# The projection's operand splits made during the gate products of the state-space stage

## The reference

```
proj = jnp.einsum('ntd,de->nte', h, lw['w_in'])
q, kc, vc, ks, vs, kw, vw, g_nsa, u, g_a, g_s = jnp.split(proj, offs, axis=-1)
...
z = jax.nn.gelu(y)
out = z * jax.nn.sigmoid(z @ w_glu.astype(f32))
```

## Time and profile before

| | us |
|---|---|
| median of 3 runs | 2201.22 |
| lowest and highest | 2199.24, 2216.53 |
| the profiled execution | 2202.53 |
| its span in the trace | 2200.7 |
| TensorE matmuls busy | 2053.4 (93%) |
| DVE, ACT, POOL busy | 904.2, 768.3, 559.5 |

### The profile page before, as it was taken

One profiled execution on the slowest core, in us unless ns is written; L12 is line 12 of the kernel. 1 busy time (PEld: TensorE's weight loads), 2 busy tenths in 40 slices (PEclk: granted clock), 3 DMA queues, 4 the chain that ended last, 5 costly groups with the idle time before them and its releaser, 6 DMA issues.

```text
span 2200.7 us, 33694 instructions
## 1 busy us (share of the span) xinstructions
PE 2053.4 (93%) x13952; PEld 1846.2 (84%) x13952; DVE 904.2 (41%) x1719; ACT 768.3 (35%) x1557; POOL 559.5 (25%) x455
## 2 busy tenths in 40 slices
PE   6998899799989999686999999999999999999997
PEld 4765599788766677455999998999999999999997
DVE  4773311166576777374211133453124214313414
ACT  5132311255466777343322232333023113202313
POOL 0640000255244444222212221122122122112120
PEclk9989899799978999798999999999999999999999
DMA  9204134465132232767111113111111111111122
GB/s 361 89 1 123 41 73 104 126 238 197 71 77 78 63 87 63 258 258 282 48 48 49 47 50 108 39 43 45 49 49 39 49 49 39 49 49 40 47 58 79
DMA packets 217072, 201.54 MB, mean 92 GB/s; under 512 B 38198, under 2 KB 199966, under 8 KB 208264
## 3 DMA queue, kind: packets, MB, share of 16 engines
q1 hardware_dynamic: 205126, 131.40, 20.9%
q0 software_dynamic: 9216, 67.11, 7.9%
q10 hardware_dynamic: 2578, 0.88, 0.2%
HBM read 177.62 MB, written 21.58 MB: 91 GB/s over the span
## 4 chain that ended last, share of the span: by engine, by line
PE 51%; DMA 1%; DVE 0%; ACT 0%; SPq 0%; issue 0%; ACTq 0%; DVEq 0%
PE ps L2230 17%; PE ps L2228 17%; PE ps L2229 17%; PE ps L2374 1%; DMA tail<-in_w_in 1%; DMA tail<-x_keep 1%; PE ps L2395 0%; DVE tail L2739 0%; ACT tail L2568 0%; DVE tail L2715 0%; SPq L2340 0%; SPq L2353 0%; ACT tail L2559 0%; DVE tail L2657 0%; ACT tail L2473 0%
## 5 line engine op out<-in xcount | busy, mean ns | idle before, releaser
L2228 PE MATMUL ps<-tail,tail 128*128 128x356 f32 (+2 forms) x2304 | 757.5, 329 | 12.3 <-POOL tail L2626 9.5
L2230 PE MATMUL ps<-tail,tail 128*128 128x356 f32 (+2 forms) x2304 | 751.1, 326 | 0.0
L2229 PE MATMUL ps<-tail,tail 128*128 128x356 f32 (+2 forms) x2304 | 749.2, 325 | 0.0
L2626 POOL TENSOR_TENSOR tail<-tail,tail 128x1024 fp32r<-128x1024 f32 x96 | 232.2, 2419 | 927.7 <-ACT tail L2473 927.7
L2228 PEld LDWEIGHTS ps<-tail,tail 128*128 128x128 f32 x2304 | 436.1, 189 | 15.3 <-POOL tail L2626 9.7
L2229 PEld LDWEIGHTS ps<-tail,tail 128*128 128x128 f32 x2304 | 436.2, 189 | 2.6 <-issue 0.2
L2230 PEld LDWEIGHTS ps<-tail,tail 128*128 128x128 f32 x2304 | 436.3, 189 | 0.0
L2473 ACT ACTIVATE tail<-tail 128x1024 fp32r<-128x1024 f32 x96 | 101.0, 1053 | 323.1 <-PE ps L2230 314.6
L2657 DVE SCALAR_TENSOR_TENSOR tail<-ps,mod,tail 128x346 f32<-128x346 f32 (+2 forms) x120 | 68.7, 572 | 347.7 <-PE ps L2230 337.7
L1683 POOL TENSOR_SCALAR pr<-pr,row_reciprocals,gT 128x640 f32<-128x640 f32 (+7 forms) x128 | 98.8, 781 | 145.0 <-DVE row_reciprocals L1809 142.4
L2528 ACT ACTIVATE tail<-tail,tail 128x346 f32<-128x346 f32 (+2 forms) x96 | 56.0, 583 | 195.5 <-DVE tail L2697 100.2
(11 more groups left out here) (492 smaller groups left out, 2987.8 us busy)
## 6 DMA issues: line engine op xcount, KB each, us to landing
tail<-in_w_ff SPq DMA_DIRECT2D x64, 512.0 KB, 3.9
wada_late<-in_w_ada SPq DMA_DIRECT2D x32, 512.0 KB, 4.1
wada<-in_w_ada SPq DMA_DIRECT2D x4, 2048.0 KB, 11.7
tail<-in_w_in SPq DMA_DIRECT2D x16, 512.0 KB, 3.7
x_keep<-xT SPq DMA_DIRECT2D x1, 4224.0 KB, 24.1
h_keep<-hT SPq DMA_DIRECT2D x1, 4224.0 KB, 13.4
tail<-x_keep SPq DMA_DIRECT2D x1, 4224.0 KB, 13.7
xrow<-in_x_prompt SPq DMA_DIRECT2D x8, 512.0 KB, 8.2
```

The costliest lines, as they stand in the source:

```text
L2228: pe.matmul(out, whi[:, kw, :], xlo(kx), start=(i == 0), stop=False)
L2229: pe.matmul(out, wlo[:, kw, :], xhi(kx), start=False, stop=False)
L2230: mm = pe.matmul(out, whi[:, kw, :], xhi(kx), start=False, stop=(i == n - 1))
L2626: pool.tensor_tensor(wlo[:, x % 2], wraw[:, x % 2], whi[:, x % 2], ALU.subtract).then_inc(w_split, 1)
```

## The change

The first split of the projection's operands moves into `stage_ssm`. SP loads the weights of items 0 and 1 there, after the last product of the state-space output is done (`y_done` at 10) and behind the store of `h_keep`. ACT, between the sigmoids of the gate, makes `h_hi` in six pieces of half the chunks by one third (after sigmoids 0 to 5) and the two `w_hi` (after sigmoids 6 and 7). DVE makes the six `h_lo` pieces and the two `w_lo` ahead of its four multiplies: one piece, three pieces, two pieces and the first `w_lo`, the second `w_lo`. New waits: ACT waits for the four stores of the states ahead of the gate; DVE waits for the store of `hT` ahead of the first `h_lo`.

The buffers `h_hi`, `w_raw`/`w_lo` and `w_hi` are placed from byte 101408 of each partition, where the state-space stage has tables that are no longer read at that time (the upper part of its scratch, `Bre` to `Fim`, `Fre` and part of `UT`); `h_lo` still takes the place of `hT`. So that the projection's own allocation begins at the same byte, `cbias` grows from 2 to 8 columns (24 bytes). In the projection the splits of `hT` and of items 0 and 1, their loads, and TensorE's waits for them are gone. The rest of the projection, and of the program, is as before.

```diff
+ROWS_OF = (2, 3, 4, 5, 0, 1)
+H_PIECES = tuple((s, k) for s in range(3) for k in (0, KD // 2))
...
             sp.dma_start(e.h_keep, e.hT[:, :, :]).then_inc(S["h_stored"], 16)
+            sp.wait_ge(S["y_done"], 8 + 2)
+            for x in range(2):
+                a = KV0 + ROWS_OF[x] * KVW
+                sp.dma_start(e.w_raw[:, x], e.w_in[0].rearrange("(k p) n -> p k n", p=P)[:, :, a:a + P]).then_inc(S["w_loaded"], 16)
             load_wait(sp, e.states_stored, 4)
...
+            load_wait(act, e.states_stored, 4)
             for i in range(12):
                 f, s = i // 3, i % 3
                 act.wait_ge(S["gate_products"], i + 1)
                 act.activation(e.ossmT[:, f, s * SL:(s + 1) * SL], bank[i % 4][:, 0:SL], ACT.Sigmoid).then_inc(S["gate_sigmoids"], 1)
+                if i < 6:
+                    s, k = H_PIECES[i]
+                    third = slice(s * SL, (s + 1) * SL)
+                    act.activation(e.hhi[:, k:k + KD // 2, third], e.hT[:, k:k + KD // 2, third], ACT.Copy).then_inc(S["h_hi"], 1)
+                elif i < 8:
+                    load_wait(act, S["w_loaded"], 2)
+                    act.activation(e.w_hi[:, i - 6], e.w_raw[:, i - 6], ACT.Copy).then_inc(S["w_hi"], 1)
...
+            load_wait(dve, S["h_stored"], 1)
             for f in range(4):
+                for i in ((0,), (1, 2, 3), (4, 5), ())[f]:
+                    s, k = H_PIECES[i]
+                    third = slice(s * SL, (s + 1) * SL)
+                    dve.wait_ge(S["h_hi"], i + 1)
+                    tt(e.hlo[:, k:k + KD // 2, third], e.hT[:, k:k + KD // 2, third], e.hhi[:, k:k + KD // 2, third], ALU.subtract).then_inc(S["h_split"], 1)
+                if f >= 2:
+                    dve.wait_ge(S["w_hi"], f - 1)
+                    tt(e.w_lo[:, f - 2], e.w_raw[:, f - 2], e.w_hi[:, f - 2], ALU.subtract).then_inc(S["w_split"], 1)
                 dve.wait_ge(S["gate_sigmoids"], 3 * f + 3)
                 tt(e.ossmT[:, f, :], e.ossmT[:, f, :], zT[:, f, :], ALU.mult).then_inc(S["gated"], 1)
...
-                pe.wait_ge(w_split, x + 1)
+                if x >= 2:
+                    pe.wait_ge(w_split, x - 1)
                 for s in range(3):
                     n = 3 * x + s
-                    if x == 0:
-                        pe.wait_ge(h_split, 2 + s)
...
-            for i, (s, k0) in enumerate(pieces):
-                a, b = span_of[s, k0]
-                act.activation(hhi[:, a:b, third(s)], e.hT[:, a:b, third(s)], ACT.Copy).then_inc(h_hi, 1)
-                if i in (1, 2):
-                    weights_hi(i - 1)
...
-            for i, (s, k0) in enumerate(pieces):
-                a, b = span_of[s, k0]
-                dve.wait_ge(h_hi, i + 1)
-                dve.tensor_tensor(hlo[:, a:b, third(s)], e.hT[:, a:b, third(s)], hhi[:, a:b, third(s)], ALU.subtract).then_inc(h_split, 1)
-                if i in (1, 2):
-                    weights_lo(i - 1)
```

More of the change, by code:

```diff
@@ L364, in stage_ssm @@
                  "toeplitz_cleared g_ready prompt_rows_kept last_states_turned sample_inputs_done lags_ready windows_moved last_power "
-                 "inputs_taken wgate_loaded head_gates_done head_gates_kept ").split()
+                 "inputs_taken wgate_loaded head_gates_done head_gates_kept h_hi h_split w_loaded w_hi w_split ").split()
         S = {n: sem(n) for n in names}
@@ L1015, in table_steps @@
     return loads, store_line, spread, loaded, clear, queries, lines, compressor_bias, near_bias, mask_row, keep_line, keep_compressor_bias, rows
-ROWS_OF = (2, 3, 4, 5, 0, 1)
+AT_SPLIT = 101408
 def stage_project(nc, e):
@@ L1028, in stage_project @@
         sem = stage_semaphores(nc, c, "proj")
[L1029 to L1032, removed]
+        assert nc.sbuf_base == AT_SPLIT, nc.sbuf_base
+        sb("split_places", [P, KD * NT + 4 * KD * P])
+        hhi, hlo, arena, whi, wlo = e.hhi, e.hlo, e.w_raw, e.w_hi, e.w_lo
         turn_in = sb("turn_in", [P, 2, NT])
@@ L1036, in stage_project @@
          t_keep_compressor_bias, t_rows) = table_steps(nc, e, sb, sem)
[L1037 to L1041, removed]
+        w_hi, w_split, products, kept, turned, rows_kept, values_laid, ones_set = (sem(n) for n in (
+            "w_hi", "w_split", "products", "kept", "turned", "rows_kept", "values_laid", "ones_set"))
         w_loaded = [sem(f"w_loaded{i}") for i in range(2)]
@@ L1049, in stage_project @@
         valid = lambda tb: P if tb < TB else NS
-        pieces = [(s, k) for s in range(3) for k in ((0, KD // 2, KD) if s == 0 else (0, KD))[:-1]]
-        span_of = {(0, 0): (0, KD // 2), (0, KD // 2): (KD // 2, KD), (1, 0): (0, KD), (2, 0): (0, KD)}
         def loads_of(x):
-            return sum(2 if NK <= y < NK + R else 1 for y in range(x % 2, x + 1, 2))
+            return sum(2 if NK <= y < NK + R else 1 for y in range(2 + x % 2, x + 1, 2))
         @block.sync
@@ L1066, in _ @@
                         sp.dma_start(arena[:, x % 2, :, g * HD:(g + 1) * HD], win[:, :, a:a + HD]).then_inc(w_loaded[x % 2], 16)
-                else:
+                elif x >= 2:
                     a = KV0 + ROWS_OF[x] * KVW
@@ L1166, in weights_lo @@
             def weights_lo(x):
-                dve.wait_ge(w_hi, x + 1)
+                dve.wait_ge(w_hi, x - 1)
                 dve.tensor_tensor(wlo[:, x % 2], arena[:, x % 2], whi[:, x % 2], ALU.subtract).then_inc(w_split, 1)
             t_mask_row(dve)
-            for i, (s, k0) in enumerate(pieces):
-                a, b = span_of[s, k0]
-                dve.wait_ge(h_hi, i + 1)
-                dve.tensor_tensor(hlo[:, a:b, third(s)], e.hT[:, a:b, third(s)], hhi[:, a:b, third(s)], ALU.subtract).then_inc(h_split, 1)
-                if i in (1, 2):
-                    weights_lo(i - 1)
             for x in range(1, NX):
@@ L2829, in stages @@
             e.gates = sb("gates", [3 * HQ, NT])
+            e.hhi = nc.alloc_sbuf_tensor_at("h_hi", [P, KD, NT], F32R, offset=AT_SPLIT)
+            e.w_raw = nc.alloc_sbuf_tensor_at("w_raw", [P, 2, KD, P], F32, offset=AT_SPLIT + KD * NT * 4)
+            e.w_lo = nc.alloc_sbuf_tensor_at("w_lo", [P, 2, KD, P], F32R, offset=AT_SPLIT + KD * NT * 4)
+            e.w_hi = nc.alloc_sbuf_tensor_at("w_hi", [P, 2, KD, P], F32R, offset=AT_SPLIT + KD * NT * 4 + 2 * KD * P * 4)
+            at_h = nc.sbuf_usable_end // 32 * 32 - (SSM // P) * NT * 4 - KD * NT * 4
+            e.hlo = nc.alloc_sbuf_tensor_at("h_lo", [P, KD, NT], F32R, offset=at_h)
             stage_ssm(nc, e)
@@ L2852, in stages @@
         e.w2 = sb2("w2c", [HD, 2, HD])
-        e.cbias = sb2("cbias", [HD, 2])
+        e.cbias = sb2("cbias", [HD, 8])
         stage_project(nc, e)
```

## The result

Twenty runs of the changed kernel have a median of 2191.27 us, twenty of the kernel before 2203.62; the ratio is 0.9956 with a 95% interval of 0.9936 to 0.9976, so 9.7 us less, between 5.3 and 14.1. The forecast was 7.7 us less, or 9.3 if TensorE's clock did not fall in the new hole. The profiled execution took 2193.91 us, with a span of 2192.1.

A forecast was written before the change was run, and what follows sets the result against it. TensorE, its matmul row busy 93% of the span, was taken as the bound, so its idle and lower-clock time counts. 6.35 + 2.91 - 1.6 = 7.66 us off 2201.22 gave 2193.5 us; range 2187 to 2200.

The forecast's parts named there:

- The start: Projection's first product on TensorE: moves from 263.22 to the barrier's end at 256.87, 6.35 us gained.
- The bound on TensorE's own start: At the barrier before the projection: TensorE is ready itself, nothing added, bound below 0.1 us.
- The clock of the first third: Projection's first 24 matmuls: the lower clock cost 6.95 - 4.04 = 2.91 us, counted as gained back.
- one short stretch: After the new 2.86 us hole at the barrier: clock at half for 3.4 us, costing 1.6 us.
- the first rival: New hole at the barrier: clock does not fall at all, 9.26 us gained, 2192.0 us; chance 0.20.
- the stretch of 2.74 us in the tail: TensorE idle before 1046.82: like case with the clock at half for about 3.4 us, used for the new hole.
- Nothing lost in the gate loop: Gate loop: copies and splits fit idle time, at least 0.58 us spare per scalar-engine slot; cost nothing.
- The fourth rival: Gate loop: copies make the scalar engine the bound once a pair exceeds 2.36 us; slower, chance 0.03.
- the mechanism named for it: Gate loop: Copy and Sigmoid need different tables, two 1.28 us loads per slot, some 15.3 us; net 2208.8.
- Through to the end: Projection onward: every microsecond gained at the front reaches the end; projection ends about 7.7 us earlier, near 399.3.
- The third rival: Later stages give the gain back through shifted low-clock stretches, 4.7 us per 10 us; 2198 to 2205, chance 0.13.
- The base: Whole kernel before the change: median of the runs, 2201.22 us, from which the gain was subtracted.

The follow-up runs named there:

- copies2: The changed kernel with each of the six h_hi copies in the gate loop made twice; 2191.98 us in its one run.
- paced: The changed kernel with ten identity products on TensorE spread over the vector engine's scans by signals; mean 2191.0 us, ratio 0.9934 to the kernel before.
- fill_hole: The kernel before with ten float32 identity products ahead of TensorE's first wait of the projection, results unused; ratio 0.9978 to the kernel before.
- copies3: The changed kernel with each of the six h_hi copies in the gate loop made three times; 2206.97 us in its one run.
- fill_y: The changed kernel with ten identity products in place of eight ahead of the y products; median 2191.65 us, ratio 0.9972 to the kernel before.
- fill_thirds: fill_y plus three identity products ahead of the turning, an earlier state-store wait, and the last gate multiply in thirds; 2187.66 us, ratio 0.9927.
- before_paced: The kernel before with ten identity products on TensorE spread over the vector engine's scans by signals; mean 2200.6 us, ratio 0.9983.
- h_only: The changed kernel with loads and splits of the first two weight items left in the projection; ratio 1.0006 to the kernel before.
- paced_all: fill_thirds with the fillers of paced and two more identity products behind the last gate product; mean 2189.2 us, ratio 0.9924 to the kernel before.

## Why the prediction held, point by point

**The start.** Predicted 6.35 us; the hole went from 9.22 to 2.92, 6.30. The bound on TensorE's own start was needed for nothing: it starts at 258.43, between SP's first issue at 258.39 and the vector engine's memset at 258.45.

**The clock of the first third.** The forecast counted 2.91 us back and then took off 1.6 for one short stretch. In the changed kernel's profile the stretch did not come, and the first rival's 9.3 us was the right sum for it (6.30 + 2.82 = 9.12 by the rows). This is the term that was mis-sized, and it is no constant: the size was right and the certainty was not. Of the six profiles with an idle stretch of 2.9 us here, the clock stayed at 1.00 in four (the changed kernel, copies2, paced, fill_hole) and went to 0.50 for 3.4 us in two (copies3, fill_y); with a stretch of 2.19 us in fill_thirds it fell all the same. Where it fell, it cost what was forecast: the first third took 5.67 us in copies3 (266.02 to its eviction at 271.69) and 5.68 in fill_thirds (254.18 to 259.86), 1.6 above the 4.04 of a third at full clock. A chance of a third to a half, so 0.5 to 0.8 us, would have been the better entry than 1.6. The row from which I took it, the stretch of 2.74 us in the tail, shows that a fall is possible, not that it is the rule.

**Nothing lost in the gate loop.** Sigmoids, multiplies, loads and waits came where the working put them: h_keep issued at 189.81, w_raw at 211.46, last w_lo at 250.12, load of item 2 issued at 270.26 with the table loads ending at 269.93. One cost was not seen: the wait for the state stores, put ahead of the first sigmoid, takes the table load with it, so that 1.28 us stands between the first gate product and its sigmoid. It costs nothing, as the next two slots have caught up, and fill_thirds, where the wait stands further ahead, has the load ahead of the gate again.

**The fourth rival was priced wrongly.** It was to decide from 0.58 us more in a slot. copies2 puts 1.40 us more into each of six slots (3.03 us, where a sigmoid and one copy back to back take 1.63) and costs nothing. Nor did the mechanism named for it appear: no table load stands between a sigmoid and a copy. The banks let TensorE run ahead and the last slots, which hold less, give the lag back; in copies2 the scalar engine works without a break to 251.1 and waits for TensorE again ahead of the sigmoid at 251.94. For six such slots the true point lies between 3.03 and 4.43 us a slot.

**Through to the end.** The 9.26 us earlier end of the projection arrived as 8.6 in the span (2200.7 to 2192.1), with the late start of 1.5 us in both; the stages behind took 0.7 us more. From the last gate product to the projection's end the profiles of before and after differ by 152.98 - 142.22 = 10.8 us, and those of before_paced and paced by 152.75 - 142.17 = 10.6. That is 1.3 to 1.7 more than 9.1 to 9.3. The later stretch at the lower clock, around the small products of the table steps, was 6.8 and 10.2 us long in those profiles of before and 3.4 us in those of after, but it was 6.8 in copies2 and 10.2 in copies3 and fill_y. A further stretch, between 368 and 386, was 6.8 us long in before, 3.4 in before_paced and 6.8 in the two of after. Together the two stretches are 3.4 us shorter in either pair, 1.6 us at 0.47 each, and that is the rest. I take their lengths for chance; no run separates it.

**The third rival, work given back later,** did not happen in any of the comparisons: from the projection's end to the end of the span the two profiles took 1793.7 and 1794.4 us. What I had read as a scatter of 17 us between three runs was two groups, with a place of its own and a cause that could be filled.

**The base.** The median of before over twenty runs is 2203.6, not the 2201.2 of three, so 2191.27 is nearer to the forecast of 2193.5 than the two gains, 12.4 us between the medians and 7.7, are to each other. That part is luck: the base was 2.4 us too low and the gain 4.7 too small, and the two errors work against each other. The gain without the groups is 9.6 us (paced against before_paced), 1.9 above the forecast and next to the 9.3 of the first rival.

## What to carry to other kernels

When several chains start together at a barrier, shortening the work is worth nothing until the longest is out: moving about four fifths of the split work (h_only) left TensorE's hole as it was and gained nothing clear of the scatter, moving the rest with it gained 9 to 10 us. A hole of TensorE costs its length and what the clock takes behind it, here another 2.8 us, so count both, and treat the second as a chance when the hole is short. And when runs of a kernel fall into two groups, look for a profile in each before averaging: here the difference was one wait elsewhere, and fillers that follow the waited-for engine removed it, where a fixed number did not.

## What the runs showed of the hardware that was not expected

The granted clock can stay at 0.50 for 41 us (about 185 to 226 in h_only) while TensorE is busy without a break. In h_only and fill_hole it fell just before the y products resumed, at an idle stretch of 3.98 and 3.99 us. In fill_y and copies3, with longer idle stretches of 6.20 and 7.88 us, it fell in the middle and was back after 6.8 us, early in the same y products. Why the same products bring it back in one case and not in the other stays open; no run here separates it.

A wait written ahead of another wait moved the automatic table load behind the first result: at 229.03 in the changed kernel, at 221.90 when the first of the two waits stands earlier in the list. The thirteen profiles agree: the load stands ahead of the first gate product's end in the five without that wait at this place (before, fill_hole, before_paced, fill_thirds, paced_all), behind it in the other eight.
